# Feed-forward gate and up slabs: high and low token parts pass a high weight tile in one 512-column matmul

## The reference

```
T = 256 tokens, D = 2048, FF = 5632
h = rmsnorm(x, norm2_gain)                        # [T, D]
a = h @ w_gate                                    # [T, FF]
a = conv_w[0]*a[t-2] + conv_w[1]*a[t-1] + conv_w[2]*a[t] + conv_b     # causal, over tokens
x = x + (silu(a) * (h @ w_up)) @ w_down
out = rmsnorm(x, final_norm_gain)
```

## Time and profile before

| what | value |
|---|---|
| median of 3 runs | 3167.4 us (3166.21 to 3169.8) |
| span of the profiled execution | 3167.3 us |
| PE busy in the span | 2711.7 us (86%) |
| DVE busy | 1737.8 us (55%) |
| ACT busy | 856.5 us (27%) |
| gate and up stage, from its first matmul to the first of the down stage | 2405.77 to 2914.29 us |
| down stage, its matmuls | 2914.29 to 3151.2 us |

### The profile page before, as it was taken

One profiled execution on the slowest core, in us unless ns is written; L12 is line 12 of the kernel. 1 busy time (PEld: TensorE's weight loads), 2 busy tenths in 40 slices (PEclk: granted clock), 3 DMA queues, 4 the chain that ended last, 5 costly groups with the idle time before them and its releaser, 6 DMA issues.

```text
span 3167.3 us, 36123 instructions
## 1 busy us (share of the span) xinstructions
PE 2711.7 (86%) x13969; PEld 2005.6 (63%) x13969; DVE 1737.8 (55%) x2146; ACT 856.5 (27%) x946; POOL 635.5 (20%) x532
## 2 busy tenths in 40 slices
PE   7999999577777777777777787999999999999998
PEld 7999779422222222222222236999778999999886
DVE  5456556855555555555555456544655545445444
ACT  3433443210000111111111003533444334433433
POOL 0000000445444444444444430000000000000000
PEclk9999999799999999999999998999999999999999
DMA  6554464899999999999999995554454555555553
GB/s 231 169 170 162 171 226 160 341 407 401 402 401 402 401 405 397 403 404 402 400 400 419 422 374 189 173 171 147 141 192 157 177 184 185 182 178 183 192 192 146
DMA packets 220042, 859.98 MB, mean 272 GB/s; under 512 B 17616, under 2 KB 20016, under 8 KB 147120
## 3 DMA queue, kind: packets, MB, share of 16 engines
q0 software_dynamic: 73728, 536.90, 41.4%
q1 hardware_dynamic: 146224, 321.79, 30.3%
HBM read 856.54 MB, written 2.10 MB: 271 GB/s over the span
## 4 chain that ended last, share of the span: by engine, by line
PE 56%; DMA 24%; DVE 12%; issue 6%; ACT 1%; POOL 1%; DVEq 0%; POOLq 0%; ACTq 0%
DMA vb<-in_peer_v,vidx 12%; DMA ub<-in_peer_u,uidx 11%; PE PS L460 10%; PE PS L462 10%; PE PS L464 10%; PE PS L1876 7%; PE PS L1736 4%; PE PS L472 4%; PE PS L476 4%; PE PS L474 4%; DVE ub L1295 3%; DVE wl L393 1%; ACT wh L388 1%; PE PS L1752 1%; POOL ub L658 1%
## 5 line engine op out<-in xcount | busy, mean ns | idle before, releaser
L1736 PE MATMUL PS<-vb,diag 128*128 128x512 f32 x1920 | 914.0, 621 | 359.3 <-DMA vb<-in_peer_v,vidx 316.9
L393 DVE TENSOR_TENSOR wl<-raw,wh 128x2048 fp32r<-128x2048 f32 x292 | 669.2, 2292 | 796.6 <-ACT wh L388 793.6
L1736 PEld LDWEIGHTS PS<-vb,diag 128*128 128x128 f32 x1920 | 356.3, 195 | 916.4 <-issue 795.0
L1295 DVE CUSTOM_DVE_ANT_0 ub<-ub,RES 128x2048 f32<-128x2048 f32 x256 | 583.1, 2291 | 498.5 <-DMA ub<-in_peer_u,uidx 498.4
L388 ACT CAST wh<-raw 128x2048 fp32r<-128x2048 f32 x292 | 555.8, 1904 | 952.3 <-PE PS L464 592.7
L460 PE MATMUL PS<-XH,wh 128*128 128x256 f32 x2816 | 800.6, 284 | 6.1 <-DVE XL L506 3.3
L462 PE MATMUL PS<-XL,wh 128*128 128x256 f32 x2816 | 797.8, 283 | 0.0
L464 PE MATMUL PS<-XH,wl 128*128 128x256 f32 x2816 | 797.7, 283 | 0.0
L460 PEld LDWEIGHTS PS<-XH,wh 128*128 128x128 f32 x2816 | 541.6, 192 | 7.8 <-issue 5.2
L462 PEld LDWEIGHTS PS<-XL,wh 128*128 128x128 f32 x2816 | 541.6, 192 | 0.1
L464 PEld LDWEIGHTS PS<-XH,wl 128*128 128x128 f32 x2816 | 541.5, 192 | 0.0
(11 more groups left out here) (295 smaller groups left out, 1479.7 us busy)
## 6 DMA issues: line engine op xcount, KB each, us to landing
raw<-in_w_in SPq DMA_DIRECT2D x112, 1024.0 KB, 5.0
raw<-in_w_ffn_gate SPq DMA_DIRECT2D x44, 1024.0 KB, 5.1
raw<-in_w_ffn_up SPq DMA_DIRECT2D x44, 1024.0 KB, 5.1
raw<-in_w_ffn_down SPq DMA_DIRECT2D x44, 1024.0 KB, 4.8
raw<-in_w_out SPq DMA_DIRECT2D x32, 1024.0 KB, 5.1
raw<-in_peer_wq SPq DMA_DIRECT2D x16, 1024.0 KB, 5.0
ub<-in_peer_u,uidx POOLq DMA_INDIRECT x256, 16.4
vb<-in_peer_v,vidx POOLq DMA_INDIRECT x240, 15.2
```

Of the source, the lines that this page charges most:

```text
L393: dve.tensor_tensor(wl[u % 2][:], raw[u][:], wh[u % 2][:].bitcast(F32), ALU.subtract).then_inc(lo_full[u % 2], 1)
L1295: dve.tensor_tensor_reduce(ub[k % RING][:], ub[k % RING][:], RES[:, tb, :], 1.0, 0.0, ALU.mult, ALU.add, dots[:, tb, k:k + 1]).then_inc(S. ...
L1736: m = pe.matmul(PS[:, 4 * tb + b, :], diag[:, k, :], vb[k % RING][:, b * W:(b + 1) * W], start=start and k == 0, stop=False, skip_group_ch ...
```

## The change

`XH` and `XL` become two halves of one buffer `XHL`, so that for each chunk of 128 rows the 256 high and the 256 low token values lie next to each other. In the gate and up slabs one matmul with 512 columns replaces the two with the high weight tile; it writes high times high into the first half of a PSUM bank and high times low into the second half. The matmul with the low weight tile keeps its 256 columns and adds into the first half. Each output tile now has a bank of its own: the gate slab fills banks 0 to 3, the up slab banks 4 to 7.

The halves are added when PSUM is emptied. ACT copies the first half of the four banks to SBUF (`FG` for gate, `FU` for up), DVE adds the second half. The third tap with its bias goes from ACT to DVE (`tensor_scalar`), and the look-back taps read `FG` in SBUF instead of PSUM. At the start of the down stage PE now waits for each PSUM half where it first writes it.

```
@@ -206,7 +206,8 @@
         a_pT = sem("a_pT")
         a_pTcp = sem("a_pTcp")
         a_out = sem("a_out")
-        ff_y = sem("ff_y")
+        ff_gate = sem("ff_gate")
+        ff_value = sem("ff_value")
         ff_conv = sem("ff_conv")
         ff_silu = sem("ff_silu")
         ff_up = sem("ff_up")
@@ -229,8 +230,8 @@
     raw = [at(f"raw{k}", 8 * k, [UC, W]) for k in range(UNITS)]
     wh = [at(f"wh{k}", 32 + 8 * k, [UC, W], F32R) for k in range(2)]
     wl = [at(f"wl{k}", 48 + 8 * k, [UC, W], F32R) for k in range(2)]
-    XH = at("XH", 64, [DC, T], F32R)
-    XL = at("XL", 80, [DC, T], F32R)
+    XHL = at("XHL", 64, [DC, 2, T], F32R)
+    XH, XL = XHL[:, :, 0, :], XHL[:, :, 1, :]
     RES = at("RES", 96, [TB, D])
     MIX = at("MIX", 112, [DC, T])
     GAIN = at("GAIN", 112, [D])
@@ -355,6 +356,8 @@
     NRM = at("NRM", PH + 32, [TB, D])
     FA = at("FA", PH, [FC, T])
     FY = at("FY", PH + 44, [4, T])
+    FG = at("FG", PH + 52, [4, T])
+    FU = at("FU", PH + 56, [4, T])
     ah = [at(f"ah{k}", PH + 48 + k, [T], F32R) for k in range(2)]
     al = [at(f"al{k}", PH + 50 + k, [T], F32R) for k in range(2)]
 
@@ -433,6 +436,34 @@
 
     def tm_out(buf):
         return PS[:, 2 * buf:2 * buf + 2, :]
+
+    def wide_out(buf):
+        return PS[:, 4 * buf:4 * buf + 4, :]
+
+    def high_out(buf):
+        return PS[:, 4 * buf:4 * buf + 4, 0:T]
+
+    def low_out(buf):
+        return PS[:, 4 * buf:4 * buf + 4, T:2 * T]
+
+    def pe_wide_slab(pe, half, buf, x_in=None):
+
+        pe.wait_ge(evac[buf], half)
+        o, low = wide_out(buf), low_out(buf)
+        for u in range(UNITS):
+            k = u % 2
+            pe.wait_ge(lo_full[k], half * 4 + buf * 2 + u // 2 + 1)
+            if x_in:
+                pe.wait_ge(x_in[0], x_in[1] + u)
+            for t in range(4):
+                for c in range(UC):
+                    x = slice(t * P, t * P + P)
+                    d = u * UC + c
+                    pe.matmul(o[:, t, :], wh[k][:, c, x], XHL[:, d, :, :].rearrange("p a n -> p (a n)"),
+                              start=d == 0, stop=False, skip_group_check=True)
+                    m = pe.matmul(low[:, t, :], wl[k][:, c, x], XH[:, d, :], start=False,
+                                  stop=d == DC - 1, skip_group_check=True)
+            m.then_inc(w_free[k], 1)
 
     def pe_slab(pe, half, buf, cm, events=None, slab=None, x_in=None):
 
@@ -968,27 +999,30 @@
 
         x_hi(act, 3)
 
-        def gate_conv(n, s):
+        def gate_copy(n, s):
 
             slab_ready(act, s)
-            if not (isinstance(n, int) and n == 0):
-                act.wait_ge(S.ff_up, n)
-            for t in range(4):
-                w2 = cols[:, 2, ds(n * 4 + t, 1)] if not isinstance(n, int) else cols[:, 2, 4 * n + t:4 * n + t + 1]
-                b = cols[:, 2, ds(n * 4 + t + FC, 1)] if not isinstance(n, int) else cols[:, 2, FC + 4 * n + t:FC + 4 * n + t + 1]
-                a = act.activation(FY[:, t, :], cm_out(0)[:, t, :], ACT.Identity, bias=b, scale=w2)
-            a.then_inc(S.ff_y, 1)
+            act.copy(FG[:], high_out(0)).then_inc(S.ff_gate, 1)
+
+        def up_copy(n, s):
+
+            slab_ready(act, s)
+            act.copy(FU[:], high_out(1)).then_inc(S.ff_value, 1)
 
         def gate_silu(n):
             act.wait_ge(S.ff_conv, n + 1)
             act.activation(FY[:], FY[:], ACT.Silu).then_inc(S.ff_silu, 1)
 
         def ff_pair(n, s, first=False):
-            for u in range(2 if first else 0, UNITS):
-                split_hi(act, s, u)
+            if not first:
+                split_hi(act, s, 0)
+                split_hi(act, s, 1)
+                up_copy(n - 1, s - 1)
+            split_hi(act, s, 2)
+            split_hi(act, s, 3)
             split_hi(act, s + 1, 0)
             split_hi(act, s + 1, 1)
-            gate_conv(n, s)
+            gate_copy(n, s)
             split_hi(act, s + 1, 2)
             gate_silu(n)
             split_hi(act, s + 1, 3)
@@ -996,13 +1030,15 @@
         ff_pair(0, S_FF, True)
         with act.Fori(1, FPAIRS) as i:
             ff_pair(i, i * 2 + S_FF)
-        def down_hi(j, s):
-            for u in range(UNITS):
+        def down_hi(j, s, u0=0, u1=UNITS):
+            for u in range(u0, u1):
                 split_hi(act, s, u)
                 act.copy(ah[u % 2][:], FA[:, ds(j * UNITS + u, 1), :].rearrange("p o n -> p (o n)")
                          if not isinstance(j, int) else FA[:, j * UNITS + u, :]).then_inc(S.ah_full, 1)
 
-        down_hi(0, S_DOWN)
+        down_hi(0, S_DOWN, 0, 1)
+        up_copy(FPAIRS - 1, S_DOWN - 1)
+        down_hi(0, S_DOWN, 1)
         act.wait_ge(S.ff_up, FPAIRS)
         with act.Fori(1, NDOWN) as i:
             down_hi(i, i + S_DOWN)
@@ -1540,21 +1576,26 @@
 
         def gate_taps(n):
 
-            dve.wait_ge(S.ff_y, n + 1)
+            dve.wait_ge(S.ff_gate, n + 1)
+            link(dve.tensor_tensor(FG[:], FG[:], low_out(0), ALU.add), evac[0])
+            for t in range(4):
+                a = dve.tensor_scalar(FY[:, t, :], FG[:, t, :], col((2, 0), n, t), col((2, FC), n, t),
+                                      ALU.mult, ALU.add)
+            link(a)
             for back, place in ((1, (1, FC)), (2, (1, 0))):
                 for t in range(4):
-                    a = dve.scalar_tensor_tensor(FY[:, t, back:], cm_out(0)[:, t, 0:T - back], col(place, n, t),
+                    a = dve.scalar_tensor_tensor(FY[:, t, back:], FG[:, t, 0:T - back], col(place, n, t),
                                                  FY[:, t, back:], ALU.mult, ALU.add)
                 link(a)
             dve.engine_nop().then_inc(S.ff_conv, 1)
-            dve.engine_nop().then_inc(evac[0], 1)
 
         def up_out(n, s):
 
-            slab_ready(dve, s)
+            dve.wait_ge(S.ff_value, n + 1)
+            link(dve.tensor_tensor(FU[:], FU[:], low_out(1), ALU.add), evac[1])
             dve.wait_ge(S.ff_silu, n + 1)
             dst = FA[:, ds(n * 4, 4), :] if not isinstance(n, int) else FA[:, 4 * n:4 * n + 4, :]
-            link(dve.tensor_tensor(dst, FY[:], cm_out(1), ALU.mult), evac[1], S.ff_up)
+            link(dve.tensor_tensor(dst, FY[:], FU[:], ALU.mult), S.ff_up)
 
         def ff_pair(n, s, first=False):
             if not first:
@@ -1571,7 +1612,7 @@
 
         ff_pair(0, S_FF, True)
         with dve.Fori(1, FPAIRS) as i:
-            link.enter(i, 1, 3)
+            link.enter(i, 1, 6)
             ff_pair(i, i * 2 + S_FF)
         link.leave(1, FPAIRS - 1)
 
@@ -1856,11 +1897,11 @@
 
         pe.wait_ge(S.mix_y, 4)
         turn_x(pe, 3, NRM)
-        pe_slab(pe, S_FF // 2, 0, True, x_in=(S.xt_lo, 29))
-        pe_slab(pe, S_FF // 2, 1, True)
+        pe_wide_slab(pe, S_FF // 2, 0, (S.xt_lo, 29))
+        pe_wide_slab(pe, S_FF // 2, 1)
         with pe.Fori(1, FPAIRS) as i:
             for k in range(2):
-                pe_slab(pe, i + S_FF // 2, k, True)
+                pe_wide_slab(pe, i + S_FF // 2, k)
 
         def down(j, s, first=False, last=False):
 
@@ -1870,6 +1911,8 @@
                 pe.wait_ge(S.al_full, j * UNITS + u + 1)
                 for tb in range(TB):
                     y = slice(tb * P, tb * P + P)
+                    if first and u == 0:
+                        pe.wait_ge(evac[tb], S_DOWN // 2)
                     for b in range(4):
                         o = PS[:, 4 * tb + b, :]
                         for n, (x, w) in enumerate(((ah, wh), (ah, wl), (al, wh))):
@@ -1880,8 +1923,6 @@
                 if not (last and u == UNITS - 1):
                     m.then_inc(w_free[k], 1)
 
-        pe.wait_ge(evac[0], S_DOWN // 2)
-        pe.wait_ge(evac[1], S_DOWN // 2)
         down(0, S_DOWN, True)
         with pe.Fori(1, NDOWN - 1) as i:
             down(i, i + S_DOWN)
```

## The result

| kernel | median | runs | range |
|---|---|---|---|
| before | 3166.8 us | 4 | 3165.8 to 3169.8 |
| changed | 3188.4 us | 4 | 3184.7 to 3195.5 |

The ratio is 1.0069, 95% interval 1.0054 to 1.0083: the change makes the kernel 21.5 us slower. Every profiled execution carries its own time; for the changed kernel it is 3184.66 us, 1.8 us over the span of 3182.9 us, and it was the fastest of the four.

A forecast was written before the change was run, and what follows sets the result against it. PE alone was taken to bound the gate and up stage. PE gain, stalls, seam and clock, -18.8 + 28.4 - 0.3 + 9.4 = +18.7 us, on 3167.4 gave 3186 us; the 8-in-10 range was 3172 to 3197 us.

The forecast's parts named there:

- The mechanism: Gate and up stage: DVE's added work ahead of up unit 2's split exceeds the slack, so PE waits once per pair.
- slack of 0.96 us: Up slab's unit 2: PE could start at 2623.76 but needs it at 2624.72, so 0.96 us to spare in every pair.
- The stalls: PE ahead of up unit 2: 2.65 us in each of ten loop pairs, 1.9 us in the first, together 28.4 us.
- The added DVE work: Ahead of up unit 2's split: one addition and four multiply-adds, together 3.2 us; bounds 2.8 and 3.5 us.
- PE's gain: Gate and up stage: two matmuls at 0.347 us replace three at 0.360 us, saving 18.8 us; bounds 0 and 18.8 us.
- one rival: Gate and up matmuls: the 13.3 ns don't go with the instruction, nothing gained on PE; +33 us, 3200 us; chance 0.06.
- an estimated 3.5 us: Gate and up stage: PE's gain from 1408 instructions less by the skill's 2.5 ns rule, giving an estimated 3198 us in sum.
- The clock: PE behind the eleven stalls: one in two followed by a low clock at 1.7 us, 9.4 us; bounds 0 and 18.7 us.
- One sign: Changed profile: the gate and up stage's windows would show a clock under 1.00.
- The clock holds: Gate and up stage: no low clock behind the stalls, so +9.3 us, 3177 us; chance 0.15.
- The seam: Start of the down stage: PE's wait for the up result goes, but unit 1's split comes later; gain 0.3 us.
- A hidden change: Split of up unit 2: DVE's added work stays within the slack, PE keeps its 18.8 us, 3149 us; chance 0.09.

The follow-up runs named there:

- The narrow matmuls in the old order of DVE: Changed kernel with the 512-column matmul taken apart into two of 256 columns, DVE's order as changed: median 3200.1 us, ratio 1.0099.
- the reordered kernel: Changed kernel with DVE's eight look-back taps behind the split of up unit 2 and ACT's SiLU behind unit 3's cast: median 3154.5 us, ratio 0.9962.
- the control: The reordered kernel with the 512-column matmul taken apart into two of 256 columns: median 3168.45 us against 3168.40 us, ratio 0.9999.
- Groups of four and four: The reordered kernel with each output tile's four 512-column matmuls first, then its four 256-column ones: median 3151.6 us, ratio 0.9950.

## Why the prediction came out right, step by step

**The mechanism held.** The slack of 0.96 us at the up slab's unit 2, DVE's added work ahead of that split, eleven stalls there and nowhere else: each shows in the profile, taking the eight taps out from ahead of the split takes the stalls away, and one more addition there makes each of them 1.05 us longer.

**The stalls were sized right.** 28.4 us were predicted. Measured are 26.2 + 11 x 0.16 = 27.9 us, and the first matmul behind each stall takes 0.11 us longer to be followed by the next, 1.2 us more. The added DVE work was put at 3.2 us and measured at 1.60 + 1.64 = 3.24 us; the bound of 2.8 us, from straight code, did not hold in the loop. In the first pair, outside the loop, the stall was 1.70 + 0.16 = 1.86 us against the predicted 1.9 us. In the loop it depends on the stretch of matmuls before it: the bracket has 2.57 to 2.61 us behind a stretch with the short value and 2.35 to 2.36 us behind a long one, 0.21 us apart, which is what two units of 16 pairs are longer at 0.0067 us a pair. The predicted 2.65 us lies between the two, 2.75 and 2.51 us with the 0.16 us. The narrow matmuls in the old order of DVE test the slack by itself, since their units are as long as before: 7.07 - 3.82 = 3.25 us of delay less 0.96 us of slack is 2.29 us, and their stalls are 2.3 us.

**PE's gain was mis-sized in the changed kernel, but not in kind.** The term of 18.8 us assumed 0.3467 us for every pair. That is what a stage shows when it has the short value throughout, though not as the sum was made up: in the reordered kernel's profile the long matmul is followed after 0.2317 us and the short one after 0.1150 us in the mean, not after 0.2267 and 0.120 us as predicted. In the profile of the changed kernel 608 pairs had the short value and 800 had 0.3533 us, which takes 800 x 0.0067 = 5.3 us off the gain. A constant 13.3 ns per instruction, read off two uniform streams, is a property of these streams; a mixed one has more than one value. That the surplus goes with the instruction at all, which one rival denied, is shown by the control: with three narrow matmuls in the same order of DVE the gain is nil, with a wide and a narrow one it is 9.4 to 18.8 us. The figure of 2.5 ns in the Trainium skill (TensorE: Matmul & The Clock Gate, "Back-to-back issue gap"), which the page gives for a matmul by itself, would have given an estimated 3.5 us. The gains measured here, each matmul with its own weight load, decide against it for this kernel.

**The clock was over-sized in the profile.** One in two stalls was taken to be followed by a low clock, 9.4 us in all. Both profiles of the changed kernel show one in eleven, and the stretch of 128 pairs behind it took 45.85 us instead of 44.48: 1.4 us. One sign that the prediction named therefore missed: the window over the stage was to show a clock under 1.00 and shows 1.00; only the 7 us behind the ninth stall show 0.76. The rival *The clock holds* had the clock more nearly right than the forecast, at 3177 us. With slightly shorter stalls (2.3 us) it was four in eleven, with longer ones (3.7 us) ten in eleven. So the size of a stall alone doesn't tell (the first of these kernels differs in its matmuls too), and two rows of the kernel before were too few for a share.

**The seam** was put at 0.3 us and measured at 0.2 us: from the stage's last step to down unit 1 6.8 against 7.0 us. The wait did not vanish but moved one unit on, as worked out.

**The sum for the profiled stage:** -18.8 + 5.3 + 27.9 + 1.2 + 1.4 = +17.0 us, as measured. That the predicted +18.7 us comes so near is in part luck: it rests on two errors that partly cancel, too much gain by 5.3 us and too much clock by 8.0 us (the falls behind the stalls, counted at 1.4 us). With the clock as measured and everything else as forecast the sum would have been +10.7 us. The median is 21.5 us slower rather than 17.9, because three of the four executions were 2 to 11 us slower than the profiled one. How much of that is long stretches and how much low clock wasn't profiled; by the measured sizes a stage with long values throughout would add 608 x 0.0067 = 4.1 us, less 5 x 0.21 us for the shorter stalls behind them, 3.0 us in all, so the slowest run needs more than that. The kernel before varies too, by 9 us over the runs that went with the experiments.

**The rivals.** A hidden change was to be faster at an added DVE work under 2.2 us; it is 3.24 us. But with the same added work ahead of the split and the eight old taps behind it that rival's result comes out: the reordered kernel reaches 3145.9 to 3161.5 us. The gain named there, 18.8 us, is the upper end; 9.4 us is the lower.

## What to carry to other kernels

Where one engine sets the pace and its helpers look half idle, work the slack out at each hand-over: a helper that is idle half of the time can still have less than 1 us to spare ahead of one instruction. Work whose result isn't needed soon belongs behind the next hand-over, not ahead of it; here the same instructions in another place turned 0.7% slower into 0.4% faster. And try the parts apart: the narrow matmuls with the new emptying of PSUM, once in the old order of DVE (+31.7 us) and once in the new one (0), tell in two runs what each half is worth.

## What the runs showed of the hardware

- The time of one pair of a 512-column and a 256-column matmul (each with its weight load) took one of two values, 0.3467 or 0.3533 us. It was constant while PE ran without a wait, up to the whole stage of 1408 pairs, and could change at a stall. The same program had the short value in three profiles (two chips) and the long one in two (a third chip), 9.4 us apart; the changed kernel had both in each of two executions. What sets it stays open. Uniform streams at full clock settled at 0.120 us for 256 columns and 0.2267 us for 512 in every profile here. Their first matmuls behind a wait or a change of size are farther apart: in the down stage of the kernel before 0.31 us for the first and 0.23 to 0.24 us for the next five. Groups of four and four gave 0.3509 us in two profiles.
- The four distances 0.120, 0.2267, 0.3467 and 0.3533 us are 9, 17, 26 and 26.5 times 13.33 ns. That is an observation; no run here tests a reason.
- The low clock (1.2 GHz) behind PE's waits isn't a matter of their length alone: 4 of 11 at 2.3 us, 2 of 22 at mostly 2.5 to 2.8 us, 10 of 11 at 2.8 to 3.8 us (in the first two groups the first stall of each profile is shorter: 1.4, 1.9 and 1.6 us). One fall cost 1.3 to 1.6 us; behind the longest waits half of the falls were about twice as long and cost 2.4 to 2.8 us.
